# Delta rule on one core: both heads' inversion products on four quarters of the array, and two element-wise steps given to GpSimd

## The reference, cut to what matters

```python
def gated_delta_rule(q, k, v, g, beta):
    G = jnp.cumsum(g, axis=-1)
    decay_mat = jnp.exp(jnp.where(causal, G[..., :, None] - G[..., None, :], -jnp.inf))
    kk = jnp.einsum('bnhrd,bnhsd->bnhrs', k, k)
    a_low = jnp.where(strict, beta[..., None] * kk * decay_mat, 0.0)
    rhs = jnp.concatenate([v * beta[..., None], k * (beta * jnp.exp(G))[..., None]], axis=-1)
    sol = lax.linalg.triangular_solve(a_low + eye, rhs, left_side=True, lower=True, unit_diagonal=True)
    u, w = sol[..., :dv], sol[..., dv:]
    qk = jnp.einsum('bnhrd,bnhsd->bnhrs', q, k) * decay_mat
    q_dec = q * jnp.exp(G)[..., None]
    k_dec = k * jnp.exp(G[..., -1:] - G)[..., None]
    def step(state, xs):
        v_new = u_c - w_c @ state
        o = q_c @ state + qk_c @ v_new
        state = state * gl_c + k_c.T @ v_new
```

## Time and profile before

| | |
|---|---|
| median of 3 runs | 2885.29 us (2885.14 to 2887.12) |
| profiled execution, its own time | 2885.75 us |
| its span in the profile | 2883.9 us |
| PE busy | 2832.7 us, 98% |
| DVE busy | 1456.6 us, 51% |
| ACT busy | 1081.3 us, 37% |
| POOL busy | 146.1 us, 5% |
| `DeltaCore` with its pipeline, in the profile's time | about 212.8 to 357.7 us |

### The profile page before, as it was taken

How to read it: one execution, slowest core, us unless ns; L and a number is a source line. 1 busy time by engine, 2 the same in 40 slices (tenths; PEclk the granted TensorE clock), 3 DMA queues, 4 the chain that set the end, 5 groups by cost and what they waited for, 6 DMA issues and landing times.

```text
span 2883.9 us, 43564 instructions
## 1 busy us (share of the span) xinstructions
PE 2832.7 (98%) x19606; PEld 2337.1 (81%) x19606; DVE 1456.6 (51%) x1431; ACT 1081.3 (37%) x1176; POOL 146.1 (5%) x74
## 2 busy tenths in 40 slices
PE   9999999999999999999999999999999998999998
PEld 7788778888888888888888888788877886888886
DVE  6676553443455544443364444466657665543432
ACT  5554542222454832222342222442235532332222
POOL 1000010000110010000110000240000000100001
PEclk9999999999999999999999999999999999999999
DMA  4220022223222022233222223322231003222232
GB/s 150 74 77 2 31 88 102 97 93 110 103 100 88 35 73 94 97 102 110 102 88 102 95 95 115 104 83 81 88 125 35 4 6 135 101 96 97 102 102 74
DMA packets 44953, 249.09 MB, mean 86 GB/s; under 512 B 8507, under 2 KB 12347, under 8 KB 17248
## 3 DMA queue, kind: packets, MB, share of 16 engines
q1 hardware_dynamic: 43616, 242.11, 24.6%
q10 hardware_dynamic: 1152, 4.19, 0.4%
HBM read 237.90 MB, written 8.39 MB: 85 GB/s over the span
## 4 chain that ended last, share of the span: by engine, by line
PE 91%; DVE 5%; ACT 3%; issue 1%; DMA 0%; SPq 0%; DVEq 0%; ACTq 0%
PE ps L667 76%; PE ps L2919 4%; PE ps L1515 1%; PE ps L2501 1%; PE ps L2211 1%; PE ps L3979 1%; PE ps L2926 1%; PE ps L2485 1%; PE ps L3962 1%; PE ps L3991 1%; PE ps L2182 0%; DVE wlo L274 0%; PE ps L3097 0%; DVE gdn_conv L1147 0%; ACT whi L268 0%
## 5 line engine op out<-in xcount | busy, mean ns | idle before, releaser
L274 DVE TENSOR_TENSOR wlo<-wraw,whi 128x2048 fp32r<-128x2048 f32 x210 | 486.6, 2317 | 911.5 <-ACT whi L268 907.3
L268 ACT ACTIVATE whi<-wraw 128x2048 fp32r<-128x2048 f32 x210 | 402.1, 1915 | 900.0 <-PE ps L667 900.0
L667 PE MATMUL ps<-ffn_xh,whi 128*128 128x512 f32 x1408 | 549.2, 390 | 0.2 <-DVE wlo L274 0.2
L667 PE MATMUL ps<-ffn_xh,wlo 128*128 128x512 f32 x1408 | 547.8, 389 | 0.0
L667 PE MATMUL ps<-ffn_xl,whi 128*128 128x512 f32 x1408 | 547.8, 389 | 0.0
L667 PEld LDWEIGHTS ps<-ffn_xh,whi 128*128 128x128 f32 x1408 | 264.3, 188 | 56.9 <-DVE wlo L274 1.0
L667 PEld LDWEIGHTS ps<-ffn_xl,whi 128*128 128x128 f32 x1408 | 264.3, 188 | 55.6 <-issue 0.7
L667 PEld LDWEIGHTS ps<-ffn_xh,wlo 128*128 128x128 f32 x1408 | 264.3, 188 | 54.9
L667 PE MATMUL ps<-ffn_uh,whi 128*128 128x512 f32 x704 | 274.1, 389 | 0.0
L667 PE MATMUL ps<-ffn_uh,wlo 128*128 128x512 f32 x704 | 273.9, 389 | 0.0
L667 PE MATMUL ps<-ffn_ul,whi 128*128 128x512 f32 x704 | 273.9, 389 | 0.0
(11 more groups left out here) (524 smaller groups left out, 4446.5 us busy)
## 6 DMA issues: line engine op xcount, KB each, us to landing
wraw<-in_weights SPq DMA_DIRECT2D x211, 1024.0 KB, 4.8
gates_kept<-gates_tmp ACTq DMA_DIRECT2D x8, 512.0 KB, 4.0
mix_gate<-gates_kept SPq DMA_DIRECT2D x8, 512.0 KB, 11.0
h<-in_x SPq DMA_DIRECT2D x4, 512.0 KB, 9.0
mix_y<-hz_kept SPq DMA_DIRECT2D x2, 1024.0 KB, 6.3
out<-out SPq DMA_DIRECT2D x4, 512.0 KB, 3.1
wraw<-in_weights SPq DMA_DIRECT2D x2, 512.0 KB, 7.4
ple_raw<-in_p SPq DMA_DIRECT2D x4, 256.0 KB, 5.1
```

The source lines that it names most:

```text
L268: c.nc.scalar.activation(c.whi[:, j % 2, :], c.wraw[:, j % 2, :], ACT.Copy).then_inc(c.hi_ready, 1)
L274: c.nc.vector.tensor_tensor(c.wlo[:, j % 2, :], c.wraw[:, j % 2, :], c.whi[:, j % 2, :].bitcast(F32), ALU.subtract).then_inc(c.lo_ready, 1)
L667: last = nc.tensor.matmul(pair[:, m, :], a, b, start=opens and n == 0 and wa + xa == 0, stop=closes and n == len(ks) - 1 and wa == 1)
```

## The change

**Products on four quarters.** The first head keeps its halves in place. The second head's XX is stored with its halves swapped (`homes`), and its products are issued by `across`, from partitions 0-63 to 64-127 and from 64-127 to 0-63. Per chunk the two heads' products now alternate over four quarters of the array. Results lie in two banks (`items`: Y_BANK-1 and Y_BANK), left products in the first 64 of each 128 columns, right products after them; so `pe_left` at level 0 waits for `attT` of both heads, which only `pe_right` did before. `Y21` goes to both halves, is copied as 128x256 instead of 64x512, and `X12` of the second head goes into MISC.

**VectorE's instructions that are split.** Since the second head's halves are swapped between X and XT, `XT0` (the subtraction from the identity), the transposes `X0` and each of the four transposes `XX` become three instructions each: 128x256, 64x256 and 64x256.

**ScalarE's.** `Xd` goes from two copies of 64x512 to four of 64x256, `X12c` from one of 64x512 to two of 64x256.

**GpSimd.** `dm` and `qd` are made by GpSimd in `pool_decays`, after `mc` of the same pair. New waits: `kS` of chunk 1 on TensorE waits for `qd`, and ScalarE waits for the last `qd` before it takes up the weight ring in the last building stage.

```diff
-                               ("dve", (... "diff", "dm qd", "AT", ...)),
-                               ("pool", ("mc",))):
+                               ("dve", (... "diff", "AT", ...)),
+                               ("pool", ("mc dm qd",))):
...
-        self.pool_mask(pool, 0)
-        pool.wait_ge(self.c.tile_done, self.j_held)
-        for p in range(1, GP):
+        for p in range(GP):
+            if p == 1:
+                pool.wait_ge(self.c.tile_done, self.j_held)
             self.pool_mask(pool, p)
+            self.pool_decays(pool, p)
+
+    def pool_decays(self, pool, p):
+        nc, D = self.c.nc, self.D[p][:, :, :]
+        pool.wait_ge(*self.at("mc", p))
+        pool.wait_ge(*self.at("diff", 2 * p + 1))
+        nc.gpsimd.tensor_tensor(D, D, self.mc[p][:, :, :], ALU.add).then_inc(*self.done("dm"))
+        pool.wait_ge(*self.at("eg", 2 * p + 1))
+        pool.wait_ge(*self.at("qn", 2 * p + 1))
+        nc.gpsimd.tensor_tensor(self.q(p), self.Q1[p][:, :, :], self.eg[p][:, :, :], ALU.mult).then_inc(*self.done("qd"))
...
+    def across(self, out, a, b):
+        for rows, other in zip(self.halves(), reversed(self.halves())):
+            last = self.c.nc.tensor.matmul(out(other), a(rows), b(rows), start=True, stop=True)
+        return last
...
+    def items(self, first, width):
+        both = self.c.ps[:, self.Y_BANK - 1:self.Y_BANK + 1, :].rearrange("p h (n t) -> p (h n) t", t=P)
+        return both[:, :, first:first + width]
...
         if what == "kS":
             pe.wait_ge(*self.at("S", 5 * p + 2 * (n - 1)))
+            if n == 1:
+                pe.wait_ge(*self.at("qd", p))
...
-            for h in range(2):
-                for n in range(NC):
-                    last = nc.tensor.matmul(Y[high, h * NC + n, :], self.Aoff[:, h, n, :], self.XX[low, 0, h, n, :],
+            for n in range(NC):
+                for h, to in enumerate((high, low)):
+                    last = nc.tensor.matmul(Y[to, n, :], self.Aoff[:, h, n, :], self.XX[low, 0, h, n, :],
...
+            second = self.chunks(self.misc(pe, self.at("X12c", k)), HALF)
...
             pe.wait_ge(*self.at("AT", 3 * k + 1))
+            pe.wait_ge(*self.at("attT", 2 * k + 1))
...
-        for h in range(2):
-            for n in range(NC):
-                last = self.both(lambda r: Y[r, h * NC + n, :], lambda r: self.Ac[r, h, n, :], lambda r: self.XX[r, 0, h, n, :])
+        for n in range(NC):
+            for h, products in enumerate((self.both, self.across)):
+                last = products(lambda r: Y[r, h * NC + n, :], lambda r: self.Ac[r, h, n, :], lambda r: self.XX[r, 0, h, n, :])
...
+                if stage == GP - 1 and s == 7:
+                    act.wait_ge(*self.at("qd", GP - 1))
...
-            nc.vector.tensor_tensor(XT, self.eye[:, None, None, :].to_broadcast([P, 2, NC, HALF]), XT, ALU.subtract)\
-                .then_inc(*self.done("XT0"))
+            for h, to, rows in self.homes():
+                eye = self.eye[rows, None, :].to_broadcast([rows.stop - rows.start, NC, HALF])
+                last = nc.vector.tensor_tensor(XT[to, h, :, :], eye, X[rows, h, :, :], ALU.subtract)
+            last.then_inc(*self.done("XT0"))
...
+    def homes(self):
+        low, high = self.halves()
+        return (0, slice(0, P), slice(0, P)), (1, low, high), (1, high, low)
...
-            nc.vector.transpose(self.both_sides(1), self.both_sides(0)).then_inc(*self.done("XX"))
+            for h, to, rows in self.homes():
+                last = nc.vector.transpose(self.head(1, h)[to, :], self.head(0, h)[rows, :])
+            last.then_inc(*self.done("XX"))
...
-        elif s == 16:
-            dve.wait_ge(*self.at("mc", p))
-            dve.wait_ge(*self.at("diff", 2 * p + 1))
-            nc.vector.tensor_tensor(self.D[p][:, :, :], self.D[p][:, :, :], self.mc[p][:, :, :], ALU.add).then_inc(*self.done("dm"))
-        elif s == 17:
-            dve.wait_ge(*self.at("eg", 2 * p + 1))
-            dve.wait_ge(*self.at("qn", 2 * p + 1))
-            nc.vector.tensor_tensor(self.q(p), self.Q1[p][:, :, :], self.eg[p][:, :, :], ALU.mult).then_inc(*self.done("qd"))
```

More of the change, by code:

```diff
@@ L1396, in __init__ @@
                                ("act", ("eg", "Dx", "vT", "kdT", "Y21c Xd X12c", "Yc", "VN", "oc osq", "oln", "ors hi")),
-                               ("dve", ("eye", "kb", "qn", "diff", "dm qd", "AT", "off XT0 X0", "attT", "X XX", "R", "S", "on og lo", "zero")),
-                               ("pool", ("mc",))):
+                               ("dve", ("eye", "kb", "qn", "diff", "AT", "off XT0 X0", "attT", "X XX", "R", "S", "on og lo", "zero")),
+                               ("pool", ("mc dm qd",))):
             for names in cycles:
@@ L1598, in pe_build @@
         elif s == 27:
+            low, high = self.halves()
+            second = self.chunks(self.misc(pe, self.at("X12c", k)), HALF)
             pe.wait_ge(*self.at("Y21c", k))
-            low, high = self.halves()
-            for h in range(2):
-                for n in range(NC):
-                    last = nc.tensor.matmul(Y[low, h * NC + n, :], self.Y[high, h, n, :], self.XX[high, 1, h, n, :],
+            for n in range(NC):
+                for h, (rows, out) in enumerate(((high, Y[low, NC + n, :]), (low, second[low, n, :]))):
+                    last = nc.tensor.matmul(out, self.joined()[rows, n, :], self.XX[rows, 1, h, n, :],
                                             start=True, stop=True)
@@ L1631, in pe_left @@
         i = LV * k + l
-        Y = self.chunks(self.bank(self.Y_BANK), HALF)
         if l:
@@ L1646, in pe_right @@
         i = LV * k + l
-        X, XT = (self.halved(self.Z_BANK + b) for b in range(2))
         pe.wait_ge(*self.at("Yc", i))
-        if l == 0:
-            pe.wait_ge(*self.at("attT", 2 * k + 1))
-        else:
+        if l:
             pe.wait_ge(*self.at("XX", i - 1))
-        for h in range(2):
-            for n in range(NC):
-                last = self.both(lambda r: X[r, h * NC + n, :], lambda r: self.XX[r, 1, h, n, :],
-                                 lambda r: self.Y[r, h, n, 0:HALF // 2])
+        X, XT, Y = self.rights(), self.turned(), self.compact()
+        for n in range(NC):
+            for h, products in enumerate((self.both, self.across)):
+                last = products(lambda r: X[r, h * NC + n, :], lambda r: self.XX[r, 1, h, n, :],
+                                lambda r: Y[r, h * NC + n, :])
         last.then_inc(*self.done("Z"))
@@ L1660, in pe_right @@
                 for n in range(NC):
-                    last = self.both(lambda r: XT[r.start:r.start + HALF // 2, h * NC + n, :],
-                                     lambda r: self.Y[r, h, n, 0:HALF // 2], lambda r: self.XX[r, 1, h, n, HALF // 2:])
+                    last = self.both(lambda r: XT[r.start:r.start + HALF // 2, n, h, :],
+                                     lambda r: Y[r, h * NC + n, :], lambda r: self.XX[r, 1, h, n, HALF // 2:])
             last.then_inc(*self.done("ZT"))
@@ L1732, in act_build @@
             act.wait_ge(*self.at("Y21", k))
[L1733 removed]
+            nc.scalar.activation(self.joined().rearrange("p n t -> p (n t)"), Y[:, 0:T // 2], ACT.Copy)\
                 .then_inc(*self.done("Y21c"))
@@ L1737, in act_build @@
                 act.wait_ge(*self.at("vn", NC * k - 1))
-            nc.scalar.activation(self.XTf[low, :, :, 0:HALF], self.XX[low, 1, :, :, :], ACT.Copy)
-            nc.scalar.activation(self.XTf[high, :, :, HALF:], self.XX[high, 1, :, :, :], ACT.Copy)\
-                .then_inc(*self.done("Xd"))
+            for h, (first, second) in enumerate(((low, high), (high, low))):
+                nc.scalar.activation(self.XTf[low, h, :, 0:HALF], self.XX[first, 1, h, :, :], ACT.Copy)
+                last = nc.scalar.activation(self.XTf[high, h, :, HALF:], self.XX[second, 1, h, :, :], ACT.Copy)
+            last.then_inc(*self.done("Xd"))
         elif s == 27:
             act.wait_ge(*self.at("X12", k))
-            nc.scalar.activation(self.XTf[low, :, :, HALF:], Y[low, :].rearrange("p (h n t) -> p h n t", h=2, n=NC), ACT.Copy,
-                                 scale=-1.0).then_inc(*self.done("X12c"))
+            for h, made in enumerate((Y[low, T // 2:], self.bank(self.MISC)[low, 0:T // 2])):
+                last = nc.scalar.activation(self.XTf[low, h, :, HALF:], self.chunks(made, HALF), ACT.Copy, scale=-1.0)
+            last.then_inc(*self.done("X12c"))
         if s in (17, 19, 21, 23):
@@ L1898, in dve_off, with head @@
             .then_inc(*self.done("AT"))
-    def both_sides(self, x):
-        return self.XX[:, x, :, :, :].rearrange("p h n t -> p (h n t)")
+    def homes(self):
+        low, high = self.halves()
+        return (0, slice(0, P), slice(0, P)), (1, low, high), (1, high, low)
+    def head(self, x, h):
+        return self.XX[:, x, h, :, :].rearrange("p n t -> p (n t)")
     def dve_right(self, dve, k, l):
         nc, i, half = self.c.nc, LV * k + l, HALF // 2
```

(2 more changed lines are left out.)

37 lines of the change are left out of this document (24 added, 13 removed).

## The result

The changed kernel takes 2899.03 us in the median of 6 runs (2897.02 to 2906.29), the kernel before 2885.74 beside it (6 runs, 2885.14 to 2890.05). The ratio is 1.0047, 95% interval 1.0034 to 1.0060. The profiled execution took 2897.56, its span 2895.7. The forecast was 2884.1, its range 2879 to 2889.

A forecast was written before the change was run, and what follows sets the result against it. TensorE's queue was taken to bound each stage's first half, mostly ScalarE's the second, with VectorE nearly full. Stages 0 to 3 gave 0.0, -0.1, -0.45 and -0.65, together -1.2 us: 2884.1 us, range 2879 to 2889.

The forecast's parts named there:

- Part 2: VectorE's split instructions: three transpositions take 1.17 us, +0.46 on 0.71, bounds +0.28 and +0.58; XT0 the same.
- the clock: TensorE's clock, 1.00 through the stretch: a fall when TensorE has gaps would prove the prediction wrong; no time given.
- Part 4: First half of stages 0 to 2: VectorE's queue takes back the products' gain; second head's diff +1.0, +0.6, +0.15 us.
- Part 6: Second half of stages 0, 1 and 2: less waiting for products, ending 1.0, 0.7 and 0.6 us earlier.
- Part 7: Stage 3, without preparation: TensorE's queue binds at first, and vn of stage 4 starts 0.65 us earlier.
- Part 1: Products on four quarters: 32 records take 0.54 us for 1.08; TensorE's busy time falls by some 26 us.
- Part 3: Level 0's wait for attT: first left product 1.6 us later in stage 1, 0.7 in 2 and 3, 1.5 in 0.
- Part 5: dm and qd on GpSimd: an addition takes 2.4 us, covered by vT before Dx; +0.0 to +0.1 us a stage.
- Rival A: First halves: VectorE doesn't bind; triples at +0.28 give a sum of -3.9 us, with slack some 2878; chance 0.18.
- B: Dx, slot 17 of stages 0 to 2: GpSimd's addition takes 4.1 us, making dm late; 2888.9 us; chance 0.12.
- C: Products: quarters don't run together for 64x32 or two quarters of one row half; 2887 to 2890 us; chance 0.08.
- D: Products: a floor of about 25 ns a record makes a group 0.80 us; 2887 us; chance 0.04.

The follow-up runs named there:

- e4: The changed kernel with XT0, X0 and XX each one whole VectorE instruction, second head computed differently (timing only): 2883.22 us, 0.9993 of the kernel before.
- e10: The changed kernel with the next pair's step (kb, qn or diff) issued ahead of the three XX transpositions on VectorE: 2894.18 us, 1.0035 of the kernel before.
- e3: The kernel before with only XT0, X0 and XX each split into three VectorE instructions, products unchanged: 2898.56 us, 1.0050 of the kernel before.
- e1: The kernel before with only dm and qd moved to GpSimd: 2885.01 us against 2884.79.
- e8: The kernel of e4 with every left and right product group issued twice: 2890.38 us, 1.0017 of the kernel before.
- e5: The changed kernel with every left and right product group issued twice: 2906.86 us, 1.0072 of the kernel before.
- e14: The changed kernel with ten idle products added to TensorE's queue in stage 0: 2901.33 us, 1.0049 of the kernel before.
- e16: The kernel before with left products of levels 1 to 4, stages 1 to 3, on four quarters and the next pair's step ahead of XX: 2881.59 us, 0.9987.
- e7: The kernel before with XT0, X0 and XX each made by two VectorE instructions over all 128 partitions, one a head: 2885.12 us, 0.9997.

## Why the prediction was wrong, point by point

Two terms of the sum failed: Part 2's price of a triple, +0.46 us where it cost +0.75, beyond the bound of +0.58, and the clock, which had no term and cost an estimated 7.6 us. The picture of Part 4 was wrong as well, though its number would have come out with the right price (below). An estimate of how they add up: the sum said -1.2 at `vn` of stage 4 and it was +14.1, so 15.3 are to be found. The clock is 7.6; 20 triples (X0 and four XX in each of four stages) at 0.29 more than priced, and four of XT0 at 0.13 more (1.32 for 0.73), are 6.3, if each counts whole. The 1.4 left over are for Parts 6 and 7 and the errors of the estimate.

**Part 1** held: the groups take 0.48 to 0.50 us, those of 64x32 records as well, and e4's stages 1 and 2 show the gain. The row of the recurrence was the right one. The floor of about 25 ns that the Trainium skill (TensorE: Matmul & The Clock Gate, "Wait — 56ns, not 53.3ns?") states does not show here either: 32 records in 0.48 us are 15 ns each. TensorE's busy time fell by 11.8 us and not by 26, in large part because at half clock its work takes longer (the windows above have some 26 us of busy time at 0.50, an estimated half of which the full clock would save).

**Part 2** failed in size. A triple takes 1.38 us from start to next start, not 1.17; against the 0.63 after which `kb` started before, that is +0.75 where I had +0.46, bound +0.58. I took overlap from two instructions over all partitions and gave it to pieces that change from one partition half to the other, which don't overlap.

**Part 3** was right in kind and short in size: the first left product of stage 2 starts 5.07 after `qk` for 3.73 (276.49 in the timeline; the chain's 276.56 is where it becomes the latest), +1.34 and not 0.7; in stage 1 5.06 for 2.88, +2.18 and not 1.6. The longer triples of XT0 and X0 are in it.

**Part 4** failed in kind. I laid VectorE's and TensorE's queues side by side and let VectorE's queue give back what TensorE won, level by level, for an end 0.15 later. Counted from `qk`, `diff` of the second head comes 1.97 later in stage 2 (19.12 for 17.15), and 2.70 later in stage 1 where 0.6 was given. The window from the first `kb` to that `diff` shows TensorE with room and VectorE with little:

```profile
288.03:300.93 12.90, 10.36 (x221) 8.60 (x223) 11.66 (x24) 2.95 (x6) 0.00 (x0) 1.00 0.01 3
```

VectorE is busy for 90% of it, as the sign asked, so its queue is nearly full. But it isn't its total that counts (e10 has the same total and another order). The levels are one serial loop: e3 shows the triple counted whole, e4 the product's gain likewise (0.36 to 0.45 a level: of the two groups only the right one is in the loop). After: -0.43 + 0.78 on the first of stage 2, 5.22 for 4.87. With Part 2's +0.46 the same loop gives -0.43 + 0.46, nothing a level, which is what I had: right by luck of the two pictures agreeing at that price, and it is the price that the changed kernel's levels show. Three levels and XT0 and X0 go into the +2.15 and +1.79 of stages 1 and 2; how they add up exactly was not worked out.

**The clock** was named among the things that would make the prediction wrong, and priced at nothing. It is no accident of one execution: the six of the changed kernel have a mean clock of 0.990 to 0.994 over the whole span, the 27 of the kernel before beside e10 one of 0.995 to 0.999. At 0.24 to 0.25 us each, the 24 us in stage 0 come to an estimated 5.9 and the 6.8 after stage 3 to 1.7, together 7.6 of the 14.1 by which `vn` of stage 4 is late (6.2 to 8.3 at 0.20 to 0.27, the lowest and the highest reading). The other 6.5 are VectorE's, less what the products won. The late part fits: from the last XX to `vn` the changed kernel takes 1.8 more than before, and e3, at 1.00 there, takes the old 5.3. For e3, 13.8 us at half clock are 3.4 of its 12.4, which leaves 9.0 for the splits with slow products. So by this estimate the faster products did win some 2.5 us over e3 (9.0 to 6.5), and the longer half clock that came with them took it back.

**Part 5** held to a tenth of a microsecond in e1. In the changed kernel GpSimd's `dm` ends when `vT` does, and `Dx` follows (timeline of stage 2):

```profile
301.77 2.36 POOL L1460 TENSOR_TENSOR gdn_D<-gdn_D,gdn_mc 128x1024 f32<-128x1024 f32 x1 [27.99 <-DVE gdn_D L1997]
...
304.16 1.06 ACT L1823 ACTIVATE gdn_D<-gdn_D 128x1024 f32<-128x1024 f32 x1
```

**Part 6** failed: from the copy of level 3 to `attT` even e4 takes 15.89 in stage 2 and 14.44 in stage 1, before 15.78 and 14.71. Instead of 0.6 and 0.7 it wins nothing and 0.27. The stretched VectorE product beside `qd` is one reason; what each of the others is worth was not tried.

**Part 7** failed too. From `qk` of stage 3 to `vn` of stage 4 the changed kernel takes 32.82 for 29.59, +3.2 and not -0.65. Of that 1.2 lie ahead of `attT` (XT0 and X0), 0.2 between there and the last XX, where the faster products and the triples about cancel (e4, with whole instructions, takes 19.30 for 22.03, the changed kernel 22.21), and 1.8 behind it, at the half clock.

**The rivals.** Rival A's condition (triples at +0.28) was the opposite of what came. B, C and D did not occur. None had the clock: the chances added up to 1 without it, and the sum of my bounds for the triples (15 x 0.12) would have given 1.8 us more.

**What stays open:** what exactly brings the clock down. A gap ahead of `qk` of 1.3 us was there in kernels that fell (e4) and that did not (before); slower VectorE work alone brought it down in e3; more products kept it up in e8 and not in e5 or e14. How VectorE's 6.5 us divide between XT0, X0 and the XX of each level, and what the gaps in e8 are, is open too.

## What to carry to other kernels

When two queues hand a buffer back and forth, follow one round of the loop through both engines before laying out either queue: each instruction on the loop counts whole, however busy or idle its engine. Price a split VectorE instruction by rows in which the pieces change partitions in the same way, and try the order that takes it off the loop (e10, e16). A change that leaves TensorE waiting more may cost its clock, be it by faster products (e4) or by slower partners (e3): put a price on that, here a fifth to a quarter of the time spent at the lower level.

## What the runs showed of the hardware

- Two 128x256 transpositions on VectorE take 0.77 us and the next instruction starts at 0.70 (e7). A piece over the low 64 partitions behind one over all 128 also starts 0.08 us early; a piece over the high half, the instruction behind it, and pieces that read one half and write the other start only when the last one has ended (e3, the changed kernel: a triple in 1.25 and 1.38 us from start to next start).
- On four quarters 32 records of 64x64 or 64x32 take 0.48 to 0.50 us, 15 ns each; at half clock 0.82 us from the first start to the last. Longer runs of them were broken in places by gaps of up to 1.07 us that no semaphore explains (e8).
- TensorE's granted clock fell to 0.50 in stage 0 right behind a gap of 2.3 us (the changed kernel), some 5 us after one of 1.3 us and 2 us after one of 0.9 (e4), and behind 1.86 and 1.70 busy us in two stretches of 2 us (e14). With the gap of 1.3 us it stayed at 1.00 in the kernel before, and with e4's two gaps in e8. A us at half clock cost 0.20 to 0.27 us in these stages.
- GpSimd's 128x1024 multiplication held up VectorE's product of the same size, 1.18 us alone, for nearly as long as the two overlapped: 0.40 us more for an overlap of 0.50 (the changed kernel), 0.72 for 0.82 (e1), 1.15 for 1.25 (e4, 2.33 in all). GpSimd's own operation took 2.37 or 2.38 us in all three.
